# Turned value products, an unnormalised first transpose, a weight unit outside the ring and a shorter router chain in a one-core decoder layer

## The reference

```python
h = rmsnorm(x, g_mix);  proj = h @ w_in            # 1024 -> 2816 columns, four branches
o_a = moba(...); o_b = diff(...); o_c = stick_breaking(...); o_d = sliding_window(...)   # 4 heads of 64 each
merged = sum_i sigmoid(h @ w_gate[i]) * (o_i @ w_br[i])
x = x + merged @ w_o
h2 = rmsnorm(x, g_ffn)                             # router: best of 4 groups, best 2 of its 8 experts
x = x + sum_experts gate_e * ((silu(h2 @ w1[e]) * (h2 @ w3[e])) @ w2[e])     # 32 experts, d_expert 512
out = rmsnorm(x, g_final)
```

## Time and profile before

| | us |
|---|---|
| median of 3 runs | 708.43 (708.27 to 709.07) |
| the profiled execution, own time | 708.31 |
| its span | 706.5 |
| PE busy, of the span | 681.2 |
| DVE busy | 246.4 |
| ACT busy | 192.7 |

### The profile page before, as it was taken

The page is one execution under the profiler, slowest core; times in us unless marked ns, Lnnn a source line. Parts: engine busy times, 40 slices in busy tenths (PEclk is TensorE's granted clock), DMA queues, the critical chain, the costliest instruction groups (busy, mean ns, idle before and its releaser), DMA issues.

```text
span 706.5 us, 9936 instructions
## 1 busy us (share of the span) xinstructions
PE 681.2 (96%) x4047; PEld 398.2 (56%) x4047; DVE 246.4 (35%) x528; ACT 192.7 (27%) x305; POOL 5.2 (1%) x9
## 2 busy tenths in 40 slices
PE   9999999999999999999999999999989898998995
PEld 6999887777777864344344344344344343453433
DVE  7563566667677772121121121121121010210212
ACT  6443565588565421110110010010010010100113
POOL 0000000000000000000000000000000000000000
PEclk9999999999999999999999999999999999999998
DMA  8897741383659959999999999999999999999994
GB/s 311 290 274 232 280 138 54 106 298 119 179 160 384 397 250 376 418 428 426 425 428 427 424 428 426 429 427 426 429 429 428 429 429 424 429 423 428 417 397 169
DMA packets 47053, 243.57 MB, mean 345 GB/s; under 512 B 10352, under 2 KB 13608, under 8 KB 33704
## 3 DMA queue, kind: packets, MB, share of 16 engines
q1 hardware_dynamic: 46568, 241.45, 85.7%
q0 software_dynamic: 448, 1.59, 0.7%
HBM read 241.96 MB, written 1.07 MB: 344 GB/s over the span
## 4 chain that ended last, share of the span: by engine, by line
PE 73%; DMA 17%; DVE 5%; ACT 2%; issue 2%; POOLq 0%; SPq 0%; DVEq 0%; ACTq 0%
PE bank L1759 25%; DMA unit<-in_w 17%; PE bank L1822 10%; PE bank L1434 7%; PE bank L1435 7%; PE bank L1436 7%; PE bank L1737 4%; PE bank L1836 2%; DVE low L340 2%; PE bank L1837 1%; PE bank L1416 1%; PE bank L1796 1%; PE bank L1769 1%; ACT prob L679 1%; PE bank L1661 1%
## 5 line engine op out<-in xcount | busy, mean ns | idle before, releaser
L1759 PE MATMUL bank<-unit,xT 128*64 128x512 f32 x1024 | 229.7, 601 | 11.4 <-DMA unit<-in_w 10.4
L1759 PEld LDWEIGHTS bank<-unit,xT 128*64 128x64 f32 x1024 | 75.8, 138 | 150.2 <-issue 144.5
L1822 PE MATMUL bank<-unit,hidT 128*64 128x512 f32 x480 | 106.3, 595 | 0.0
L1434 PE MATMUL bank<-high,hT_hi 128*128 128x512 f32 (+2 forms) x208 | 79.7, 383 | 1.6 <-DVE low L340 1.1
L1435 PE MATMUL bank<-low,hT_hi 128*128 128x512 f32 (+2 forms) x208 | 77.4, 372 | 0.0
L340 DVE TENSOR_TENSOR low<-unit,high 128x2048 fp32r<-128x2048 f32 (+1 forms) x34 | 70.7, 2098 | 10.3 <-ACT high L335 10.2
L1822 PEld LDWEIGHTS bank<-unit,hidT 128*64 128x64 f32 x480 | 33.1, 137 | 61.5 <-issue 60.0
L1436 PE MATMUL bank<-high,hT_lo 128*128 128x512 f32 (+2 forms) x176 | 65.1, 370 | 0.0
L335 ACT ACTIVATE high<-unit 128x2048 fp32r<-128x2048 f32 (+1 forms) x34 | 59.1, 1758 | 14.6 <-DMA unit<-in_w_in 12.0
L1311 DVE TENSOR_TENSOR y_lo<-bank,y_hi 128x512 fp32r<-128x512 f32 x30 | 20.8, 692 | 94.1 <-ACT y_hi L823 94.1
L1737 PEld LDWEIGHTS bank<-pick,hk 128*128 128x128 bf16 x768 | 44.4, 98 | 13.5 <-issue 12.2
(11 more groups left out here) (253 smaller groups left out, 681.4 us busy)
## 6 DMA issues: line engine op xcount, KB each, us to landing
unit<-in_w SPq DMA_DIRECT2D x80, 2048.0 KB, 30.4
unit<-in_w SPq DMA_DIRECT2D x24, 1024.0 KB, 10.9
unit<-in_w_gate SPq DMA_DIRECT2D x8, 2048.0 KB, 9.9
unit<-in_w SPq DMA_DIRECT2D x12, 512.0 KB, 15.8
unit<-in_w_in SPq DMA_DIRECT2D x2, 2048.0 KB, 18.0
unit<-in_w_o SPq DMA_DIRECT2D x2, 2048.0 KB, 10.6
unit<-in_w_in SPq DMA_DIRECT2D x6, 512.0 KB, 7.6
unit<-in_w_in SPq DMA_DIRECT2D x3, 1024.0 KB, 12.1
```

Of the source, the lines that this page charges most:

```text
L1434: mm(dst, a_hi, b_hi, start=first, stop=False)
L1759: last = mm(bank[4 + w][g * CAP:(g + 1) * CAP, :], xT[:, k, g * CAP:(g + 1) * CAP], rhs, start=(k == 0), stop=(k == KD - 1))
L1822: last = mm(bank[6 + n][g * CAP:(g + 1) * CAP, :], hidT[:, c, g * CAP:(g + 1) * CAP], rhs[:, c, n * BANK:(n + 1) * BANK], start=(c == 0), ...
```

## The change

- The first transposes read `x` itself; the row norms are worked out beside them. They are put in later: on the rows of V blocks by ACT, on the columns of T blocks by DVE (with a turned copy of the norms made by two matmuls), and in the gates through the scale of `Tanh`. T blocks all leave through DVE, V blocks through ACT. `keep_warm` is 10 before the transposes (23 before) and 6 after them (3 and 2 before).
- For A, C and D the value product gives the output turned: two heads at a time, 64 PSUM rows each (`values_of_two`). The softmax is normalised before the transposes of `middle` (`weights_of_head`), not at the output; `head_output` and the transposes of `turn` stay for B alone. There are two buffers for the turned weights. `branch(1, 0)` moves to step 9, and in D `low_part` goes ahead of `merge`.
- Unit 3 lies outside the ring, in three places (1/4 where `hid` and `hidT` will be, 1/4 where `remainder` was, 1/2 where the first rows of `x` were), loaded in three transfers during the router. The ring holds ten others. `gfin` is loaded after it, ahead of the experts' ring.
- The router's group choice loses three operations and gains one, `slot` loses one, `third_part(3)` and `ge` come after `picks`, and the first half of the first gather (`gather_first`) reads the late piece last.
- The w2 of the last but one pair comes in halves, that of the last pair in quarters of its second column half; `combine(p - 1, [0])` moves into the last `up` with w1; the last parts of `down` alternate by row group.
- At the end the squares of token tile 1 are taken by DVE (`bn_stats`), POOL's scaling goes to ACT, and ACT issues one of the four stores.

```diff
-HALVED = (8, 9)
-IN_PARTS = range(10, 18)
+HALVED = (9, 10)
+IN_PARTS = range(11, 18)
+SPARE = 3
...
-               (0, 4, 0, 0, 2), (0, 4, 0, 2, 4), (0, 4, 1, 0, 2), (0, 4, 1, 2, 3), (0, 4, 1, 3, 4))
+               (0, 4, 0, 0, 2), (0, 4, 0, 2, 4), (0, 4, 1, 0, 1), (0, 4, 1, 1, 2), (0, 4, 1, 2, 3), (0, 4, 1, 3, 4))
...
+        def held_before(n):
+            turn = turn_of(n) - RING
+            return turn + (turn >= SPARE)
...
-            sp.dma_start(x[:, 0, :], a["x"][0, 0:P, :]).then_inc(s_x[0], 16)
-            sp.dma_start(cst[:, 0:C_GE], a["constants"][:, 0:C_GE]).then_inc(s["cst"], 16)
-            sp.dma_start(x[:, 1, :], a["x"][0, P:TOK, :]).then_inc(s_x[1], 16)
+            sp.dma_start(ident, a["constants"][:, C_ID:C_ID + P]).then_inc(s["cst"], 16)
+            for t in range(NT):
+                sp.dma_start(x[:, t, :], a["x"][0, t * P:(t + 1) * P, :]).then_inc(s_x[t], 16)
             sp.dma_start(gmix[:], a["g_mix"][0].rearrange("(p k) -> p k", k=KD)).then_inc(s["cst"], 16)
...
+            spare_source = expert_source(SPARE, 0)
+            sp.wait_ge(s["lg_ps"], NT)
+            sp.dma_start(spare_last[:], spare_source[:, 6:8, :]).then_inc(s["spare"], 16)
+            sp.wait_ge(s["parts3"], 2 * NT)
+            sp.dma_start(spare_third[:], spare_source[:, 4:6, :]).then_inc(s["spare"], 16)
+            sp.wait_ge(s["absorbed"], 1)
+            sp.dma_start(spare_first[:], spare_source[:, 0:4, :]).then_inc(s["spare"], 16)
+            sp.wait_ge(s["pos"], 1)
+            sp.dma_start(gfin[:], a["g_final"].partition_broadcast(P)).then_inc(s["late"], 16)
...
-            for units_of, read in (((10, 11), 1), ((12, 13), 2), ((14, 15), 3), ((16, 17), 4)):
+            for units_of, read in (((11, 12), 1), ((13,), 2), ((14, 15), 3), ((16, 17), 4)):
...
+            def weights_of_head(st):
+                ...
+                link(nc.vector.reciprocal(lsum[:, par, 0, :], lsum[:, par, 0, :]))
+                for t, (c0, c1) in enumerate(TILE_COLS):
+                    last = nc.vector.tensor_scalar(prob[par][:, 0, c0:c1], prob[par][:, 0, c0:c1], lsum[:, par, 0, t:t + 1],
+                                                   None, ALU.mult)
+                last.then_inc(s["probs"], 1)
...
-            link(V.scalar_tensor_tensor(out=cg[:], in0=ge[:], scalar=0.0, in1=from_end(NG), op0=ALU.is_equal, op1=ALU.mult))
+            for t in range(NT):
+                last = V.scalar_tensor_tensor(out=cg[:, t, :], in0=lg[:, t, 0:NG], scalar=m[:, 0, t:t + 1], in1=group_rank[:],
+                                              op0=ALU.is_equal, op1=ALU.mult)
+            link(last)
             link(V.tensor_reduce(m[:, 1, :], cg[:], AX, ALU.max))
-            link(V.tensor_tensor(ohg[:], cg[:], t4(m[:, 1, :]), ALU.is_equal))
-            link(V.tensor_scalar(ohg[:], ohg[:], -1.0, NEG, ALU.add, ALU.mult))
...
-            third_part(3)
             dve.wait_ge(s["pos"], 1)
-            link(V.scalar_tensor_tensor(out=slot[:], in0=bank[5][:, 0:NT * NE].rearrange("p (t e) -> p t e", t=NT),
-                                        scalar=1.0, in1=asg[:], op0=ALU.add, op1=ALU.mult))
-            link(V.tensor_scalar(slot[:], slot[:], -1.0, None, ALU.add))
+            link(V.tensor_tensor(slot[:], bank[5][:, 0:NT * NE].rearrange("p (t e) -> p t e", t=NT), asg[:], ALU.mult))
...
-            keep_warm(23)
+            keep_warm(10)
             pe.wait_ge(s["cst"], 32)
             for t in range(NT):
+                pe.wait_ge(s_x[t], 16)
                 for k in range(KD):
-                    if k % 4 == 0:
-                        pe.wait_ge(s["hk"], t * (1 + k // 4) + 1)
...
-                keep_warm((3, 2)[t])
+            keep_warm(6)
...
+            def values_of_two(st):
+                ...
+                for keys in range(NT):
+                    dst = turned_part(b, h // 2)[:, keys * P:]
+                    cols = slice(0, TOK) if keys == 0 else slice(TOK, MAP)
+                    for head in (st - 1, st):
+                        c = V_AT[b] + (D_HEADS[head % 4] // 2 if b == D_ else head % 4) * HD
+                        rows = slice((head % 2) * HD, (head % 2) * HD + HD)
+                        last = mm(dst[rows, :], vv[:, keys, c:c + HD], turned_weights(head)[:, cols],
+                                  start=(keys == 0), stop=(keys == NT - 1), skip_group_check=True)
+                last.then_inc(s["pv"], 1)
...
-                gather(main, 0, half, first=True)
+            pe.wait_ge(main["P"], 1)
+            gather_first()
+            gather(main, 0, 1, first=True)
```

More of the change, by code:

```diff
@@ L449, in load_expert_unit @@
             def load_expert_unit(n, i=0, loop=False):
-                if n < RING and not loop:
+                if n <= RING and not loop:
                     k = slot_of(n)
@@ L553, in _ @@
             count = PAIRS * PAIR_UNITS
-            for n in range(head + LOOPS * span, count - PIECED * PAIR_UNITS):
+            for n in range(head + LOOPS * span, count - PAIR_UNITS - 2):
                 load_expert_unit(n)
-            sp.wait_ge(s["pos"], 1)
-            sp.dma_start(gfin[:], a["g_final"].partition_broadcast(P)).then_inc(s["late"], 16)
             for i, (before_last, r, n_half, k0, k1) in enumerate(LAST_PIECES):
@@ L915, in _ @@
                 last.then_inc(s["hTl"], 1)
+            dve.wait_ge(s["rms"], NT)
+            link(nc.vector.reciprocal(rs[:], rs[:]))
+            nc.vector.tensor_scalar(rs_half, rs[:], 0.5, None, ALU.mult)
+            for t in range(NT):
+                last = nc.vector.tensor_scalar(rs_cols(t), ident, 0.0, rs[:, t:t + 1], ALU.mult, ALU.add)
+            last.then_inc(s["norms"], 1)
             for half in range(2):
                 low_part(dve, nc.vector, 1, half)
+            dve.wait_ge(s["row_norms"], 1)
+            nc.vector.tensor_copy(rs_rows, bank[7][:, 0:TOK]).then_inc(s["row_norms"], 1)
+            dve.wait_ge(s["row_norms"], 2)
             def bias_vectors():
@@ L1091, in _ @@
                 ahead = st + 1 if st < 15 else None
+                if b in (B_, D_) and h == 0:
+                    turned(b - 1)
                 if ahead:
@@ L1558, in gate_half @@
                 for k in range(4 * half, 4 * half + 4):
-                    last = three(bank[4 + st % 2][:], hT_hi[:, k, rows], hT_lo[:, k, rows], hi[:, k, :], lo[:, k, :],
+                    last = three(gate_bank(st)[:], hT_hi[:, k, rows], hT_lo[:, k, rows], hi[:, k, :], lo[:, k, :],
                                  k == 0, k == KD - 1)
@@ L1747, in gather, with up @@
                 gather_half(z, p, half)
-            def up(w, z, p, slots, here, first=False, reads=()):
-                if not first:
+            def up(w, z, p, slots, here, first=False, reads=(), ks=range(KD)):
+                if not first and ks[0] == 0:
                     pe.wait_ge((z["hT"], z["ST"])[w], p)
-                for k in range(KD):
+                for k in ks:
                     if k % 4 == 0:
@@ L1825, in down @@
                         last.then_inc(z["Y"], 1)
-                    elif by_halves and step == CE + 1:
+                    elif tell and step == CE + 1:
                         last.then_inc(s["part_read"], 1)
@@ L1870, in experts @@
                     gather(main, p + 1, 1)
-                    down(main, p, slots, here, by_halves=base == 0)
+                    down(main, p, slots, here, by_halves=base == 0 or before_last == 1, tell=base == 0)
                 else:
-                    pe.wait_ge(main["y0"], p)
+                    combine(main, p - 1, [0])
+                    up(0, main, p, slots, here, ks=range(KD // 2, KD))
                     turn_picks(main, p)
-                    combine(main, p - 1, [0])
                     up(1, main, p, slots, here)
```

421 lines of the change are left out of this document (231 added, 190 removed), and 1 row of the table LAST_PIECES.

## The result

The changed kernel takes 702.92 us (median of 4 runs, 702.47 to 703.28); the kernel before took 708.45 beside it. That is 5.5 us less by the medians. The ratio, taken from executions timed beside each other, is 0.9916, interval 0.9904 to 0.9929, or 6.0 us less (5.0 to 6.8). 8.6 was forecast.

What follows compares the result with a forecast made beforehand. The weight stream bounds the pairs, TensorE the stretch ahead of them. Start +1.2, attention -5.0, router chain -0.9, spare unit with `gfin` -3.1 and end -0.8 sum to -8.6: 708.31 becomes 699.7 us, range 695.5 to 704.5.

Steps and rivals of the forecast that it cites:

- start: Transposes and first projection: fewer `keep_warm` matmuls let TensorE stand and perhaps run slow, and norm turning adds matmuls; plus 1.2 us.
- attention: Attention on TensorE: value products of two heads overlap, three turns go, waits shrink; minus 5.0 us.
- router chain: Router up to the first `up`: fewer group and `slot` operations, `third_part(3)` off the path; minus 0.9 us.
- unit outside the ring: Weight stream: unit 3 fills the hole, but a second hole of 3 us leaves 2.0 of its 4.9 us.
- `gfin`: Weight stream: the final gain vector moves into the hole, so 512 KB less follow it; 1.2 us gained.
- end: Kernel's tail: finer last pieces 0.3 and an earlier last store issue 0.5; minus 0.8 us.
- The low level in the transposes: Start: after TensorE's standstill the transposes likely run at 1.2 GHz, 0.26 us each instead of 0.13.
- Rival 1: Start: TensorE stays at 1.2 GHz through the transposes and into the projections, 2.1 us more, 701.8; chance 0.14.
- rival for "slower": Start: TensorE stays at 1.2 GHz through the whole first unit, adding 11.4 us, 711.1; chance 0.04.
- rival 2: Attention: DVE takes TensorE's place as the bound, so attention gives 1 us instead of 5, 703.8; chance 0.15.
- Rival 3: Weight stream: second hole absent or short, spare unit gives its whole 4.9 us, attention 6; 696.6; chance 0.12.
- The end of the kernel follows the end of the stream: Whole expert stretch: the stream's end, set by ring fill start, hole length and bytes left after it, sets the kernel's end.

Runs made afterwards that it cites:

- the last experiment: Changed kernel with each `keep_warm` matmul written as four of 128 columns, and unit 3 back in the ring; 702.50 us, ratio 0.9909.
- `gfin` late: Changed kernel with the final gain vector loaded after all whole units, as in the kernel before; 703.45 us, ratio 0.9921.
- narrow `keep_warm`: Changed kernel with its 16 `keep_warm` matmuls of 512 columns written as 64 of 128, 96 instructions more on TensorE; 701.50 us, ratio 0.9888.
- the padded one: Changed kernel with 160 waits on a long-arrived semaphore (80 instructions) on TensorE ahead of the first gather; 710.46 us, ratio 1.0023.
- two `keep_warm`: Changed kernel with 176 waits ahead of the first gather and 2 `keep_warm` matmuls instead of 10 before the transposes; one execution, 713.71 us.
- the two kernels of before that were slowed: Kernel before with 260 waits (130 instructions) ahead of its first gather, 724.65 us; and with 28 `keep_warm` matmuls written as 112 narrow ones, 710.51 us.

## Why the forecast was right in direction and 3 us too good

| step | forecast | measured | from |
|---|---|---|---|
| start | +1.2 | -0.4 | second unit's first product 22.22, before 22.58; other executions -0.7 to +1.0 |
| attention | -5.0 | -4.3 | first turn of `merged` 221.11 to 216.44, less the start |
| router chain | -0.9 | -0.7 | that turn to the first `up` |
| unit outside the ring | -1.9 | -1.9 | pair 14 in the last experiment; 1.5 and 1.7 by the times |
| `gfin` | -1.2 | 0 to -0.4 | `gfin` late |
| end | -0.8 | 0 | last matmul to end of span 6.7 before and after |
| code loaded again in the loop | not in the sum | +2.0 | narrow `keep_warm`, in three pairs of kernels |

The measured terms make -5.3 to -5.7, against 5.5 by the medians and 6.0 by the ratio. That they agree so well is partly luck, since terms read in single executions stand beside terms from ratios. And that the total was only 3 us off is luck in part too: the start was 1.6 better than forecast, which hid as much of what `gfin`, the end and the attention fell short (2.3 to 2.7) and of the 2.0 that was in no term.

**Start.** The term was too high by 1.6, in the changed kernel's profiled execution. `gmix` landed at 6.70, not 7.6 (it had taken 5.5 in the earlier trace rows and took 4.6 now), and the transposes ran at the high level, by their pace of 0.13 us each:

```profile
6.75 2.05 PE L1478 MATMUL bank<-cst,x 128*128 128x128 f32 x16 [1.22 <-DMA gmix<-in_g_mix]
...
10.18 1.15 PE L1521 MATMUL bank<-hT_hi,high 128*128 128x256 f32 x8
```

The low level in the transposes, which the forecast thought likely, is what other executions show. With ten (or 40 narrow) matmuls ahead, 16 transposes took 2.05 us in six executions and 3.43 to 3.68 in four; the stand before them was 0.7 to 1.5 us in the first and 1.0 to 2.0 in the others. The profile's clock column reads 1.00 over the first 12 us of all but one of them, even where a `keep_warm` matmul takes its slow 0.43, so the level there is read from durations. That one, of the last experiment, has 0.50 from 8 to 10 us:

```profile
6.76 3.43 PE L1470 MATMUL bank<-cst,x 128*128 128x128 f32 x16 [2.01 <-DMA gmix<-in_g_mix]
```

That is 0.21 a transpose, where the prediction took 0.26. In these four the first projection was at 11.0 to 11.6, near the forecast's 11.9, and the second unit's first product at 23.05 to 23.54, 0.5 to 1.0 later than before. Rival 1, the low level on into the projections and 2.1 more, came in no execution: the first group of eight took 1.15 to 1.29 us in all of them. In no run did the low level last through the first unit, so the rival for "slower" has nothing behind it. The rule of the Trainium skill that the prediction weighed (TensorE: Matmul & The Clock Gate, "PE-mode transpose") has transposes not counting as activity. No run here decides on it: the level was high from the first transpose in six executions, after ten matmuls (or 40 narrow ones), and no run had transposes with no matmuls before them.

**Attention.** The value products of two heads take 0.80 on the chain, not the 0.66 taken from `up`: they save 2.3 of the 3.1. Three turns at 0.5 save 1.5. TensorE's idle time from 100 to 225 us went from 3.6 to 3.2, the net 0.4 that was forecast; DVE did not take its place (rival 2). These sum to 4.2 of the 4.3.

**The unit outside the ring.** The working held: hole filled, new one at 277, and 1.9 of the 4.9 arrives at pair 14, where 2.0 was worked out. Rival 3 (no second hole) is out.

**`gfin` and the end: two terms of the sum that failed.** "The end of the kernel follows the end of the stream" is true for units up to pair 14's w1, not behind it. From 639.72 to the last `down` at 684.62 TensorE works through 44.9 us in which no unit is late. `gfin` was queued behind the last whole units in the kernel before, so it delayed only pieces that had the time. The end's term counted to the last issue of a store. That did come earlier, but what ends the kernel is the transfer of the stores, and it did not. The end of the changed kernel:

```profile
694.81 0.70 DVE L1446 BATCH_NORM_STATS2 row_stats<-bank 128x6 f32<-128x512 f32 x1 [0.85 <-PE bank L1898]
...
696.45 1.39 DVE L1456 SCALAR_TENSOR_TENSOR xg<-bank,rs,gfin 128x512 f32<-128x512 f32 x2
...
696.97 1.33 SPq L642 DMA_DIRECT2D out<-xg  x3
697.59 0.39 ACTq L916 DMA_DIRECT2D out<-xg  x1
```

From the last matmul (694.78) to the first scaling, ACT's at 696.24, it is 1.46 us; before it was 1.27 (699.79 to 701.06). The first store is issued 2.2 after the last matmul (before 2.1), and the last issue ends 3.5 after it instead of 4.3. But in both kernels DMA moves the 1 MB of the four stores from 3.0 to 5.9 us after the last matmul (697.8 to 700.7, before 702.7 to 705.7), and the span ends 6.7 after it. The 0.8 won at the last issue goes in waiting for the transfer: the store from ACT lands 2.9 after its issue where those of before took 2.2. The 0.3 for the pieces did not come either: from the start of the last `down` to the last matmul it is 10.2 us, before 10.1.

**What no step of the prediction had.** The change shortens TensorE's code ahead of the loop (34 matmuls fewer in the program, 97 instructions in all). The loop thereby begins elsewhere, and its body, which had stayed loaded from the first run to the second, is loaded again. This is shown both ways: 96 instructions more in the changed kernel win 2.0 us, the same 96 without the spare unit 2.2, 168 more in the kernel before lose 2.1, and in each case packets and gap go together with the time. The Trainium skill (Advanced Engine Details and Errata, "ISA Cache") gives TensorE 128 KB of instruction cache in lines of 16 KB, 256 instructions. The packets agree: 6 are 0.10 MB, and eight instructions decide between none and seven.

Why the place decides is my reading of this rule, not shown by itself. In the assembled programs the body is some 1665 instructions, 6.5 lines of 256, so it touches seven lines or eight, by where it begins. It begins at instruction 3831 before, 3830 in the narrow warm kernel and 3814 in the padded one, and these do not load it again; it begins at 3734 in the changed kernel, 3806 with two `keep_warm`, 3961 and 3999 in the two kernels of before that were slowed, and these do. All fourteen kernels fit one rule, that a body on seven lines stays and one on eight is loaded again, if a line begins between 3807 and 3814. Where the lines lie no trace shows, nor why eight, which would just fill 128 KB, should be too many.

How the 2 us come about is shown in part. The gap of 2.7 can't be all of it: TensorE waits for DMA from 550 us on and would have stood later for what it stood here. Nor is it the low clock, which two kernels with the gap did not have, one of them 2.1 us slower all the same. By 640 us the queue of units had moved 221.48 MB in the changed kernel and 221.84 in the narrow warm one, 0.8 us of stream; without the spare unit it was 220.75 and 220.72, no loss. The start of pair 14 differs by 2.9 in the first of these pairs and by 0.8 in the second, or 1.7 counted from the first `up`. The rest is then in the landing of single units. That a unit's last part comes later when code is loaded between would fit; it was not tested.

## What to carry to other kernels

Read the queue for instructions during a loop's second run. If it moves packets there and a shorter or longer program ahead of the loop does not, the loop's place costs time: 0.3% here. It can be moved with instructions that take no time: narrower `keep_warm` matmuls did that, waits with nothing to wait for did not. Ask of every transfer that is moved away which wait behind it still ends on DMA: a stream's total matters only up to the last unit that is waited for.

## What the hardware showed that I had not expected

- Waits on a semaphore that has long arrived are not free: TensorE stood 7.66 us for 160 of them and 12.96 us for 260, 0.05 us a wait or 0.1 an instruction.
- After a wait of about 2.2 us for DMA the next `up` takes 8.78 us instead of 7.09 in some cases and not in others: after 2.19 it took 8.77 at 643.95 (before; granted clock 0.51 in its first 3.45 us) and 7.09 at 580.82 (narrow warm without the spare unit; clock 1.00); after 2.73 at 639.72 it took 7.09. The gap at the loop's edge does the same: 8.78 after 2.69, 7.09 after 2.72. At pair 14, where nothing absorbs it, TensorE's path to the last `down` was 44.9 us without it and 46.0 with it (in the changed kernel's form; 45.7 with it in the kernel before). The changed kernel happened to be spared in its profiled execution; the kernel before and the narrow warm one were not.
